# Matrix memory of a decoder step: the states of two samples worked on together, updates alternating between two row groups, stores and loads in pairs

## The reference, cut to what matters

```python
num = s @ v + inter * (q @ c_prev)                 # per sample and head
den = sum(s) + inter * (q @ n_prev)
h = num / maximum(abs(den), exp(-m_t))
wk = w * k
c_new = decay * c_prev + wk.T @ v                  # 512 x 512 floats
n_new = decay * n_prev + sum(wk)
```

## Time and profile before

| | |
|---|---|
| Time before, median of 3 runs | 1632.83 us (1629.47 to 1633.82) |
| The profiled execution's own time | 1633.13 us |
| Its span, first to last instruction | 1631.4 us |
| TensorE busy | 1349.5 us (83%) |
| VectorE busy | 531.0 us (33%) |
| Granted TensorE clock, mean | 0.913 |
| Bytes moved | 532.80 MB, mean 327 GB/s |
| State loads and stores (lines 311, 343) | 32 + 32 of 1024 KB |

### The profile page before, as it was taken

One profiled execution on the slowest core, in us unless ns is written; L12 is line 12 of the kernel. 1 busy time (PEld: TensorE's weight loads), 2 busy tenths in 40 slices (PEclk: granted clock), 3 DMA queues, 4 the chain that ended last, 5 costly groups with the idle time before them and its releaser, 6 DMA issues.

```text
span 1631.4 us, 18559 instructions
## 1 busy us (share of the span) xinstructions
PE 1349.5 (83%) x7619; PEld 760.5 (47%) x7622; DVE 531.0 (33%) x1229; ACT 195.1 (12%) x425; POOL 31.8 (2%) x66
## 2 busy tenths in 40 slices
PE   8998999998999856865866899999997666855867
PEld 5654333376764422422432477777543323422424
DVE  5546766735032220220220323640322202211222
ACT  2233223110020000000000111200200000000001
POOL 4000000000000000000000000000000000000000
PEclk8998999998999987988987999999999889888979
DMA  7232999994727999999999974543499999999994
GB/s 208 104 104 63 402 392 392 378 340 171 292 104 311 427 427 429 428 427 429 429 428 429 410 272 140 176 188 128 168 421 429 427 427 428 429 427 429 428 429 194
DMA packets 101341, 532.80 MB, mean 327 GB/s; under 512 B 6410, under 2 KB 24010, under 8 KB 76366
## 3 DMA queue, kind: packets, MB, share of 16 engines
q1 hardware_dynamic: 97472, 526.25, 79.5%
q10 hardware_dynamic: 3360, 5.09, 1.0%
q0 software_dynamic: 448, 0.62, 0.2%
HBM read 492.45 MB, written 39.49 MB: 326 GB/s over the span
## 4 chain that ended last, share of the span: by engine, by line
PE 53%; DMA 28%; DVE 7%; issue 2%; SPq 1%; ACT 1%; DVEq 0%
DMA arena<-in_moe_w_up 28%; PE bank L899 19%; PE bank L1277 10%; PE bank L1299 5%; PE bank L1257 3%; PE bank L1312 3%; PE bank L1030 2%; DVE arena L1662 2%; PE bank L1182 1%; PE bank L1285 1%; PE bank L1191 1%; SPq L390 1%; ACT arena L769 1%; DVE arena L1607 1%; PE bank L993 1%
## 5 line engine op out<-in xcount | busy, mean ns | idle before, releaser
L1277 PE MATMUL bank<-arena,hT 128*32 128x512 f32 x2048 | 263.4, 672 | 197.8 <-DMA arena<-in_moe_w_up 185.6
L899 PE MATMUL bank<-hT,arena 128*128 128x288 f32 x1024 | 260.8, 414 | 3.3 <-DVE hT L1475 3.3
L1277 PEld LDWEIGHTS bank<-arena,hT 128*32 128x32 f32 x2048 | 78.8, 122 | 369.1 <-issue 368.1
L899 PEld LDWEIGHTS bank<-hT,arena 128*128 128x128 f32 x1024 | 195.0, 193 | 62.5 <-ACT arena L574 4.2
L1822 DVE TENSOR_TENSOR arena<-arena,bank 64x512 f32<-64x512 f32 x32 | 22.1, 692 | 531.7 <-ACT arena L769 531.7
L1257 PE MATMUL bank<-arena 128*128 128x128 f32 (+1 forms) x864 | 153.8, 308 | 1.2 <-DVE arena L1797 0.9
L1299 PE MATMUL bank<-arena 128*32 128x512 f32 x1024 | 129.1, 648 | 21.3 <-DVE arena L1826 21.3
L1257 PEld LDWEIGHTS bank<-arena 128*128 128x128 f32 (+1 forms) x864 | 117.3, 187 | 48.7 <-issue 14.4
L899 PE MATMUL bank<-arena 128*128 128x288 f32 x512 | 130.4, 415 | 0.0
L899 PEld LDWEIGHTS bank<-arena 128*128 128x128 f32 x512 | 97.7, 193 | 31.7 <-issue 3.5
L769 ACT ACTIVATE arena<-bank 64x512 f32<-64x512 f32 x32 | 18.8, 588 | 755.3 <-PE bank L1277 755.3
(11 more groups left out here) (352 smaller groups left out, 1027.8 us busy)
## 6 DMA issues: line engine op xcount, KB each, us to landing
arena<-in_moe_w_gate SPq DMA_DIRECT2D x64, 2048.0 KB, 29.8
arena<-in_moe_w_up SPq DMA_DIRECT2D x64, 2048.0 KB, 32.1
arena<-in_moe_w_down SPq DMA_DIRECT2D x64, 2048.0 KB, 25.2
arena<-in_state_mlstm_C SPq DMA_DIRECT2D x32, 1024.0 KB, 8.5
out_C_s<-arena SPq DMA_DIRECT2D x32, 1024.0 KB, 10.5
arena<-in_mlstm_w_up SPq DMA_DIRECT2D x8, 2048.0 KB, 11.4
arena<-in_cmlp_w_in SPq DMA_DIRECT2D x8, 2048.0 KB, 17.1
arena<-in_mlstm_w_down SPq DMA_DIRECT2D x4, 2048.0 KB, 18.0
```

The source lines that it names most:

```text
L899: ins = mm(B[m % 4][:, 0:NT], w[:, k, 128 * i:128 * i + 128], rhs(k), start=(k == 0), stop=(k == kt - 1))
L1277: ins = mm(B[j][CAP * i:CAP * i + CAP, :], xq[h][:, k, CAP * e:CAP * e + CAP], w[i][:, k, :], start=(k == 0), stop=(k == KD - 1), skip_gro ...
```

## The change

The states of two samples, b even and b + 1, are worked on together. TensorE computes the numerators of both, then the updates in two halves: parts 0 and 1 of both states, alternating between them, then `between` for the even sample; parts 2 and 3 of both, alternating, then `between` for the odd one. Since the two samples stand in neighbouring groups of 32 partitions, neighbouring updates read different row groups, and go to different banks as before. `update_number` numbers the updates in the new order, and VectorE merges in that order, the first four of a pair where it merged the even state, the last four where it merged the odd one. The even state is complete at the seventh merge of the pair, the odd one at the eighth. SyncE stores both, then waits for each store and issues the load that takes its place. ScalarE's copy of bank 4 waits for the 25th update of the head instead of the 29th, which is now the first behind the last numerators.

```diff
+        def update_number(h, b, i):
+
+            return MH * (NB * h + b - b % 2) + 2 * i + b % 2
+
...
-            for q in range(NB * H + 1):
-                if q < NB * H:
-                    sp.wait_ge(s("c_new"), MH * (q + 1))
-                    sp.dma_start(state(O["C_s"], q), cview(q)).then_inc(s(f"c_stored{q % 2}"), 16)
-                if q > 0:
-
-                    r = q - 1
+            for q in range(0, NB * H, 2):
+                for r in (q, q + 1):
+                    sp.wait_ge(s("c_new"), MH * q + 2 * MH - 1 + r % 2)
+                    sp.dma_start(state(O["C_s"], r), cview(r)).then_inc(s(f"c_stored{r % 2}"), 16)
+                for r in (q, q + 1):
                     sp.wait_ge(s(f"c_stored{r % 2}"), 16 * (r // 2 + 1))
                     if r + 6 < NB * H:
                         load_state(r + 6)
...
-                act.wait_ge(s("c_mm"), 32 * h + 29)
+                act.wait_ge(s("c_mm"), 32 * h + 25)
...
-                for b in range(NB):
-                    q = NB * h + b
-                    pe.wait_ge(s(f"c_landed{q % 6}"), 16 * (q // 6 + 1))
-                    for i in range(MH):
-                        mm(B[4][NS * i:NS * i + NS, :], qz[:, i, NS * b:NS * b + NS], cview(q)[:, i, :],
-                           start=(b == 0), stop=(b == NB - 1), skip_group_check=True)
-                    if b % 4 == 0:
-                        pe.wait_ge(s("parts"), 8 * h + 4 + b)
-                    g = 32 * (b % 4)
-                    for i in range(MH):
-                        n = MH * q + i
-                        if n >= 4:
-                            pe.wait_ge(s("c_new"), n - 3)
-                        mm(B[UPD[n % 4]][:, :], wk8[g:g + 32, b // 4, 128 * i:128 * i + 128], v8[g:g + 32, b // 4, :],
-                           start=True, stop=True).then_inc(s("c_mm"), 1)
-                    between(h, b)
+                for pair in range(NB // 2):
+                    two = (2 * pair, 2 * pair + 1)
+                    for b in two:
+                        q = NB * h + b
+                        pe.wait_ge(s(f"c_landed{q % 6}"), 16 * (q // 6 + 1))
+                        for i in range(MH):
+                            mm(B[4][NS * i:NS * i + NS, :], qz[:, i, NS * b:NS * b + NS], cview(q)[:, i, :],
+                               start=(b == 0), stop=(b == NB - 1), skip_group_check=True)
+                    if pair % 2 == 0:
+                        pe.wait_ge(s("parts"), 8 * h + 4 + 2 * pair)
+                    for half in range(2):
+                        for i in (2 * half, 2 * half + 1):
+                            for b in two:
+                                n = update_number(h, b, i)
+                                g = 32 * (b % 4)
+                                if n >= 4:
+                                    pe.wait_ge(s("c_new"), n - 3)
+                                mm(B[UPD[n % 4]][:, :], wk8[g:g + 32, b // 4, 128 * i:128 * i + 128],
+                                   v8[g:g + 32, b // 4, :], start=True, stop=True).then_inc(s("c_mm"), 1)
+                        between(h, two[half])
...
-                    for i in range(MH):
-                        c = cview(NB * h + b)[:, i, :]
-                        n = (NB * h + b) * MH + i
+                    for i, b2 in ((i, b2) for i in (b % 2 * 2, b % 2 * 2 + 1) for b2 in (b - b % 2, b - b % 2 + 1)):
+                        c = cview(NB * h + b2)[:, i, :]
+                        n = update_number(h, b2, i)
                         dve.wait_ge(s("c_mm"), n + 1)
-                        stt(c, c, decb[:, h, b:b + 1], B[UPD[n % 4]][:, :], ALU.mult, ALU.add).then_inc(s("c_new"), 1)
+                        stt(c, c, decb[:, h, b2:b2 + 1], B[UPD[n % 4]][:, :], ALU.mult, ALU.add).then_inc(s("c_new"), 1)
```

## The result

The changed kernel takes 1657.46 us (median of 4 runs, 1656.72 to 1658.36) against 1632.57 of the kernel before in the same session: a ratio of 1.0153, 95% interval 1.0137 to 1.0170. It is slower by 24.9 us; the forecast was 1630 in a range of 1624 to 1643. The profiled execution has a span of 1656.6 us, 25.2 more than before. The z product starts at 349.31 us, not at 323.43: 25.9 later. All of the loss is in the state stage.

A forecast was written before the change was run, and what follows sets the result against it. The prediction took TensorE and VectorE to bound the state stage, with DMA nearly full beside them. Its terms, -3.9 + 3.0 - 1.7 = -2.6 us, gave 1630 us, in a range of 1624 to 1643.

The forecast's parts named there:

- The bound of the kernel before: State stage: the chain alternates between TensorE and VectorE; DMA is nearly full beside it, with 2% of room.
- Updates alternate: State stage, heads 0 to 2: row groups overlap, saving 0.43 us in three groups per head, -3.9 us.
- Both numerators first: Start of heads 1 to 3: the first update, which VectorE waits for, comes 1.0 us later; +3.0 us.
- Last head: Last head of the state stage: earlier merges and numerators beside them, against later first updates; together -1.7 us.
- Head 0: First head: overlapping updates save 1.3 us; the later first update costs 0, hidden by TensorE's 2.97 us wait.
- The sum: State stage: -3.9 + 3.0 - 1.7 = -2.6 us, giving 1630 us; chance of this forecast 0.39.
- The clock: Rival, behind each head's denominators: four stretches at granted clock 0.50 go, 6.8 us more saved, 1624 to 1626; chance 0.15.
- No overlap: Rival, state updates: row groups do not overlap when each update waits and signals for itself; +1.3 us, 1634; chance 0.07.
- Stores and loads: SyncE's queue in the state stage: the same 64 transfers reordered cost 0 while each load lands before its numerators.
- L: State stage: time DMA loses per pair of states, between 0.2 and 1.3 us, taken as 0.4; hidden up to 0.53.
- DMA becomes the bound: Rival, state stage: with L = 1.3 late loads make z start 7.4 us later, 1640 us; chance 0.37.
- The row that was taken: Trace at 323.45, only one store queued behind the finished one: 361 GB/s for 2 us, 0.2 us lost.

The follow-up runs named there:

- a quarter of the stores: Kernel before, with only the first of four 128-row parts of each updated state stored: 1631.96 us, ratio 0.9998.
- the two kernels in halves: Changed kernel with stores and loads of half states, issued as soon as merged: 1629.99 us; the same without alternating updates: 1633.67 us.
- the two light kernels: Kernel before and changed kernel, each storing only one of four parts of every updated state: 1631.96 and 1629.33 us.
- the old order: Changed kernel with SyncE storing, waiting and loading state by state as before: 1647.57 us; without alternation 1647.06, and with the even store early too 1636.49.

## Why the prediction was wrong

- **The bound of the kernel before** was read rightly: a quarter of the stores changes its time by -0.5 us.
- **Updates alternate**: the spacing, 0.53, is exact, and 0.44 less in each of nine groups is the predicted 3.9. The 3.7 between the two kernels in halves is no clean check of it: 5.6 by the last head's start, 2.7 of it lost there in a wait for transfers. That it comes so near is in part luck. The Trainium skill's rule that tiling speeds up TensorE but not the emptying of PSUM (page TensorEngine Tiling (Array Packing), section PSUM Bottleneck) did not take the gain here; the trace agrees with the prediction's reading that VectorE is idle ahead of these groups.
- **Both numerators first**: +1.0 per head at its start. From the numerators' start to the merges it is 2.22 us (187.99 to 190.21), 1.35 before: +0.87. Right.
- **Last head**: -1.7 predicted, beside the 0.87 at its start. With a quarter stored the head takes 0.9 more, so nothing is left of it. Yet from the last update of its first two states to the denominators the head gains 2.5 us (293.01 to 305.34 before, 289.01 to 298.80 after), and the numerators of b = 7 cost 0.87: -1.7, as predicted. Behind that, matmuls that TensorE did at a granted clock of 1.00 fall into a stretch at 0.50 (310.73 to 314.14), which takes 1.7 back. In the two light kernels, before and then after:

```profile
315.57 1.81 PE bank L1049 x4
317.38 0.86 PE bank L1060 x2
```
```profile
309.89 2.65 PE bank L1051 x4
312.54 1.71 PE bank L1062 x2
```

- **Head 0** gains 3.3 us in these kernels, where 1.3 was predicted. In its first part the granted clock is 0.50 for 3.4 us less (143.61 to 157.26 before, 146.89 to 157.13 after); how much of the 2.0 us that makes is not shown.
- **The sum** of TensorE and VectorE, -2.6, came out at -2.6 in the medians and -4.0 at z's start. By heads it is -3.3, -0.7, -0.9 and +0.9, against -1.3, -0.3, -0.3 and -0.7: the terms hold roughly, and that the medians match exactly is luck.
- **The clock**: the rival's sign came and its gain did not. Behind the denominators the granted clock is 1.00 in all four heads of the changed kernel (here in head 1, where the earlier trace rows has 0.50):

```profile
223.42 1.13 PE L1114 MATMUL bank<-arena 128*128 128x512 f32 x2
224.38 1.02 PE L1116 MATMUL bank<-arena 128*128 128x512 f32 x2
```

  But stretches at 0.50 stand elsewhere. Over the state stage the mean granted clock is 0.92 in both light kernels, and 0.83 in the changed kernel, where TensorE stands in waits. The prediction reckoned with stretches that go or come, not with stretches that move.
- **No overlap** fell by the spacing.
- **Stores and loads**: here it failed. The step is "That is less than the 2.6 us of the store left behind, so the queue should not run dry", with L between 0.2 and 1.3 us per pair and 0.4 taken. Load 31 lands at 334.69, and its numerators start then:

```profile
334.73 1.06 PE bank L1186 x8
...
349.31 38.80 PE bank L901 x160
```

  By the prediction's own formula 302.2 + 13 L = 334.7, so L is 2.5, as the two holes have it. The rival "DMA becomes the bound" was right in kind, and its 1.3 half the size. The step took the store behind as 2.6 us of work still to be done when the awaited one is reported; in head 1 the run shows 0.01 MB moved in half a microsecond then, by one engine. That is the first hole, 0.9 us a pair on the mean. The second, 1.5 us a pair, the prediction does not have at all.
- **The row that was taken**: 323.45 stood for the case that fits in full. There the sixteen counts of the awaited store came within 0.5 us (322.94 to 323.43). In the row that was set aside they were 2.4 us apart (310.02 to 312.40), as at 203.99 in the changed kernel. That engines can run ahead and out of work was written there, for a deeper queue only; it happens in the shallow one too. And 323.45 is one event at the end of the stage, where 13 pairs follow on each other.
- The Trainium skill's fixed cost of about 2.0 us (page DMA: Bandwidth & Descriptors, section Anatomy of one DMA) is measured there on transfers that GpSimd issues; these are issued by SyncE. Cited in the prediction with L = 0, it misled in the same way: the trace does not agree, at 2.5.
- The prediction priced the late even store only as a delay of the first pair (some 8 us). That it also lets SyncE stand in a wait with nothing to issue at every head's start was missed: 10.6 us in the old order.

## What to carry to other kernels

An in-order queue that stores, waits and reloads must have work queued behind the transfer that it waits for, counted not from the transfer's end but from when most of its engines end; one equal transfer behind was too little here, a transfer and a half in smaller pieces nearly enough. Where work is grouped in pairs, keep the queue's old order, or a finer grain: the gain of the pairs (2.6 us) was in the compute engines, and the loss in the order of the queue that went with it, which costs the kernel before 26 us when it alone is changed. Before such a change, look not at the mean rate of a stage alone but at the windows just behind each wait of the queue, and at all such waits: the one row that spoke for no loss was the untypical one.

## What the runs showed of the hardware that was not expected

In head 1 the report of a 1 MB store came when another 1 MB queued behind it was nearly moved: one of sixteen counts was 0.9 to 1.7 us behind the fifteenth in three pairs, and at 204.00 the rate was 74 and then 29 GB/s in the first microsecond after the report, 160 in the next, 377 in the third. Behind the second report of a pair the engines were busy and still moved only 232 to 291 GB/s. Stretches at a granted clock of 0.50 moved from one place in a head to another when the order of the work changed, and in the kernels with a quarter stored the mean over the stage stayed at 0.92. Twice as many transfers of half the size cost nothing that can be seen: 391 GB/s over a head with 0.52 MB each, 393 with 1.05 MB.
